# DeltaNet output norm and the second branch merge made one stage, in a one-core hybrid encoder kernel

## The reference, cut to what matters

```
o_b, s_gdn_new = gdn_recurrence(qb, kb, vb, beta, log_g, s_gdn)
o_b = rmsnorm(o_b, p['gdn_norm_w']) * jax.nn.silu(gb.reshape(B, T, GDN_HEADS, GDN_DV).astype(f32))
y_b = o_b.reshape(B, T, GDN_V).astype(h.dtype) @ p['w_br_b']
g_a, g_b, g_c = jnp.split(jax.nn.sigmoid(h @ p['w_gate'] + p['b_gate']), 3, axis=-1)
out = (g_a * y_a + g_b * y_b + g_c * y_c) @ p['w_out']
```

## Time and profile before

| | us |
|---|---|
| median of three runs | 2665.25 |
| lowest and highest run | 2663.41, 2666.01 |
| span of the profiled execution (its own time) | 2667.1 |
| TensorE busy | 2248.3 (84%) |
| VectorE busy | 758.6 (28%) |
| ScalarE busy | 417.9 (16%) |
| GpSimd busy | 188.9 (7%) |

### The profile page before, as it was taken

One profiled execution on the slowest core, in us unless ns is written; L12 is line 12 of the kernel. 1 busy time (PEld: TensorE's weight loads), 2 busy tenths in 40 slices (PEclk: granted clock), 3 DMA queues, 4 the chain that ended last, 5 costly groups with the idle time before them and its releaser, 6 DMA issues. The chain is left out here.

```text
span 2667.1 us, 27006 instructions
## 1 busy us (share of the span) xinstructions
PE 2248.3 (84%) x10591; PEld 1501.7 (56%) x10591; DVE 758.6 (28%) x1560; ACT 417.9 (16%) x929; POOL 188.9 (7%) x225
## 2 busy tenths in 40 slices
PE   4928698989999699799838999949969928999985
PEld 2215565755544466466417888836634417788772
DVE  1115265021020611023393444421113331111116
ACT  3001211110031400011222111140001101111112
POOL 0000000000000000000002211100000030000005
PEclk9968798579999899899968999969989969999997
DMA  6620212211200111111510000011141009999976
GB/s 223 224 40 2 35 34 14 1 48 40 58 0 0 29 29 40 20 32 40 9 1 16 9 9 1 1 36 36 35 162 56 32 13 354 350 351 353 348 259 215
DMA packets 227881, 237.03 MB, mean 89 GB/s; under 512 B 64976, under 2 KB 186160, under 8 KB 227776
## 3 DMA queue, kind: packets, MB, share of 16 engines
q1 hardware_dynamic: 218916, 206.32, 27.5%
q0 software_dynamic: 8880, 29.51, 3.0%
HBM read 207.87 MB, written 26.62 MB: 88 GB/s over the span
## 5 line engine op out<-in xcount | busy, mean ns | idle before, releaser
L2428 PEld LDWEIGHTS ex_ps<-ex_xt,ex_w_in 128*128 128x128 f32 x2048 | 236.0, 194 | 18.4 <-issue 14.8
L2428 PE MATMUL ex_ps<-ex_xt,ex_w_in 128*128 128x128 f32 x2048 | 236.3, 277 | 3.2 <-DMA ex_w_in<-in_w_exp_up 3.2
L1402 PE MATMUL cv_ps<-h,cv_w 128*128 128x364 f32 (+1 forms) x576 | 177.9, 472 | 17.1 <-DMA cv_w<-in_w_in 17.1
L1402 PEld LDWEIGHTS cv_ps<-h,cv_w 128*128 128x128 f32 x576 | 110.1, 192 | 83.9 <-DMA cv_w<-in_w_in 17.7
L2076 PE MATMUL pj_ps<-pj_w_out,mix 128*128 128x512 f32 (+1 forms) x288 | 127.0, 600 | 23.5 <-DMA pj_w_out<-in_w_out 23.5
L927 PE MATMUL b_gate_ps<-h,b_merge_w 128*128 128x364 f32 (+1 forms) x384 | 122.7, 473 | 7.1 <-DMA b_merge_w<-in_w_br_b 7.1
L927 PE MATMUL a_gate_ps<-h,a_merge_w 128*128 128x364 f32 (+1 forms) x384 | 122.9, 474 | 6.6 <-DMA a_merge_w<-in_w_br_a 6.6
L2439 PE MATMUL ex_ps<-ex_w_down,ex_hid 128*128 128x512 f32 x256 | 118.2, 605 | 8.1 <-DVE ex_hid L2514 5.9
L675 PE MATMUL s_ps<-h,s_w_gate 128*128 128x364 f32 (+1 forms) x384 | 117.3, 468 | 0.8 <-ACT s_before L726 0.8
L2076 PEld LDWEIGHTS pj_ps<-pj_w_out,mix 128*128 128x128 f32 (+1 forms) x288 | 53.2, 187 | 92.0 <-issue 67.9
L927 PEld LDWEIGHTS b_gate_ps<-h,b_merge_w 128*128 128x128 f32 x384 | 73.7, 192 | 51.8 <-DMA b_merge_w<-in_w_br_b 7.2
(11 more groups left out here) (442 smaller groups left out, 3095.1 us busy)
## 6 DMA issues: line engine op xcount, KB each, us to landing
ex_w_in<-in_w_exp_gate SPq DMA_DIRECT2D x32, 1024.0 KB, 8.3
ex_w_in<-in_w_exp_up SPq DMA_DIRECT2D x32, 1024.0 KB, 10.9
ex_w_down<-in_w_exp_down SPq DMA_DIRECT2D x32, 1024.0 KB, 9.9
ada_w<-in_w_ada SPq DMA_DIRECT2D x12, 2048.0 KB, 7.9
ys_dram<-ex_y SPq DMA_DIRECT2D x32, 512.0 KB, 10.0
cv_w<-in_w_in SPq DMA_DIRECT2D x12, 512.0 KB, 4.5
x_tiles<-in_x_prompt SPq DMA_DIRECT2D x1, 4096.0 KB, 15.5
s_w_gate<-in_w_gate SPq DMA_DIRECT2D x8, 512.0 KB, 3.9
```

What stands on the lines that cost most here:

```text
L1402: last = nc.tensor.matmul(ps[n][:, 0:width], w[:, j % 2, k], g.h[:, k, at:at + width], start=k == 0, stop=k == KD - 1)
L2428: last = nc.tensor.matmul(ps[2 + b][:, P * m:P * m + P], w_in[:, b, m // 2, k, P * (m % 2):P * (m % 2) + P], xt[:, b, k], start=m == 0 and ...
```

## The change

The two stages `stage_gdn_out` and `stage_merge` for branch B become one, `stage_gdn_merge`, with one barrier fewer. Its instructions are those of the two stages, with these differences. The 36 squares with their sums move into the core: ScalarE takes those of tile i-2 in tile i between the second decay exp and the power2 copies, and those of tiles 7 and 8 at its end. They write to `g.row_sel` and to the space of `g.gdn_ba`. The core's weight tile `w_gate` outlives it, and SP loads the first two column blocks of the merge's gate weights into it when gate jobs 27 and 36 are done. In the new stage ScalarE takes the root first and Silu after it. TensorE does the gate products of block 0, pieces 0 and 1, then the 9 transposes, then piece 2, then the branch products of block 0. Blocks 1 to 7 are written out without a loop, in the order of before. Gate and branch weights have buffers of their own; the gate weights of j are loaded after the gate products of j-2, branch weights after its branch products. The transposes use five PSUM banks, three of them those of the branch products.

```diff
         q_state = x[1]
         state = [sb(f"state{b}") for b in range(2)]
-        w_gate = sb("w_gate", [P, 2, KD, P])
+        w_gate = g.w_gate
+        square = g.row_sel[:, 0:P]
...
                 sp.dma_start(w_gate[:, c % 2], gate_view[:, :, P * c:P * c + P]).then_inc(S[f"gate_w{c % 2}"], 16)
+            merge_view = rows_view(d["w_gate"][0])[:, :, D:2 * D]
+            for j in range(2):
+                sp.wait_ge(S["gate_psum"], NT * (j + 3))
+                sp.dma_start(w_gate[:, j], merge_view[:, :, P * j:P * j + P]).then_inc(g.merge_loaded[j], 16)
...
+            def sum_squares(i):
+                n = P if i < NT - 1 else CHUNK
+                act.wait_ge(S["o_out"], i + 1)
+                for h in range(HEADS):
+                    q = HEADS * i + h
+                    if q:
+                        act.wait_ge(S["squared"], q)
+                    nc.scalar.activation(square[0:n], g.gdn_v[0:n, i, DV * h:DV * h + DV], ACT.Square,
+                                         accum_out=g.gdn_ssq[0:n, q:q + 1]).then_inc(S["squared"], 1)
+
             for i in range(NT):
...
                 nc.scalar.activation(decay[:], ps[2][:], ACT.Exp).then_inc(S["dec_exp"], 1)
+                if i >= 2:
+                    sum_squares(i - 2)
                 for r, (to, bank) in enumerate(((power2, 2), (power2_t, 3))):
...
+            sum_squares(NT - 2)
+            sum_squares(NT - 1)
...
+def stage_gdn_merge(nc, g, d):
...
+            def load_br(j):
+                sp.dma_start(w_br[:, j % 2], br_view[:, :, P * j:P * j + P]).then_inc(br_loaded[j % 2], 16)
+
+            sp.dma_start(bias[:], d["b_gate"][0].rearrange("(b k p) -> b p k", p=P, b=3)[1],
+                         allow_slow_non_contiguous=True).then_inc(bias_loaded, 16)
+            sp.dma_start(norm_col[:], d["gdn_norm_w"][0].rearrange("(p o) -> p o", o=1), allow_slow_non_contiguous=True).then_inc(loaded, 16)
+            load_br(0)
+            load_br(1)
+            for j in range(2, KD):
+                sp.wait_ge(gate_psum, 3 * (j - 1))
+                sp.dma_start(g.w_gate[:, j % 2], gate_view[:, :, D + P * j:D + P * j + P]).then_inc(g.merge_loaded[j % 2], 16)
+                sp.wait_ge(br_psum, 3 * (j - 1))
+                load_br(j)
+
+        @block.tensor
+        def _(pe):
+            def gates(j, n):
+                at, width = PIECES[n]
+                if n == 0:
+                    pe.wait_ge(g.merge_loaded[j % 2], 16 * (j // 2 + 1))
+                if j:
+                    pe.wait_ge(gate_done, 3 * (j - 1) + n + 1)
+                for k in range(KD):
+                    last = nc.tensor.matmul(gate_ps[n][:, 0:width], g.w_gate[:, j % 2, k], g.h[:, k, at:at + width],
+                                            start=k == 0, stop=k == KD - 1)
+                last.then_inc(gate_psum, 1)
+
...
+            def turn(i):
+                n = tokens(i)
+                pe.wait_ge(gated_o, i + 1)
+                if i >= 5:
+                    pe.wait_ge(branch_done, i - 4)
+                for h in range(HEADS):
+                    last = nc.tensor.transpose(turn_ps[i % 5][:, P * h:P * h + n], g.gdn_v[0:n, i, DV * h:DV * h + DV], g.ident[0:n, 0:n])
+                last.then_inc(turned, 1)
+
+            gates(0, 0)
+            gates(0, 1)
+            for i in range(NT):
+                turn(i)
+            gates(0, 2)
+            pe.wait_ge(branch_done, NT)
+            for n in range(3):
+                branch(0, n)
+            for j in range(1, KD):
+                for n in range(3):
+                    gates(j, n)
+                    branch(j, n)
+
+        @block.scalar
+        def _(act):
+            act.wait_ge(pads, 1)
+            nc.scalar.activation(std[:], g.gdn_ssq, ACT.Sqrt, scale=1.0 / DV, bias=g.eps[:]).then_inc(std_done, 1)
+            for i in range(NT):
+                nc.scalar.activation(swish[:, i], g.gate_rows(i), ACT.Silu).then_inc(swish_done, 1)
+
+            def sigmoid(j, n):
+                at, width = PIECES[n]
+                act.wait_ge(gate_psum, 3 * j + n + 1)
+                if j:
+                    act.wait_ge(gated, 3 * (j - 1) + n + 1)
+                nc.scalar.activation(gate[:, n, 0:width], gate_ps[n][:, 0:width], ACT.Sigmoid, bias=bias[:, j:j + 1]).then_inc(gate_done, 1)
+
+            act.wait_ge(loaded, 16)
+            for i in range(NT):
+                n = tokens(i)
+                act.wait_ge(turned, i + 1)
+                act.wait_ge(swish_done, NT)
+                nc.scalar.activation(g.branch[:, :, P * i:P * i + n], turn_ps[i % 5][:].rearrange("p (h t) -> p h t", h=HEADS)[:, :, 0:n],
+                                     ACT.Copy, scale=norm_col[:, 0:1]).then_inc(branch_done, 1)
+            act.wait_ge(bias_loaded, 16)
+            for j in range(KD):
+                for n in range(3):
+                    sigmoid(j, n)
+
...
+            g.gdn_ssq = g.gdn_ba[:].rearrange("p i c -> p (i c)")[:, 0:NT * HEADS]
             stage_gdn_in(nc, g, d, out)
+            g.w_gate = sb("gdn_w_gate", [P, 2, KD, P], inner)
+            g.merge_loaded = [inner.enter_context(nc.semaphore(f"merge_b_loaded{b}")) for b in range(2)]
             stage_gdn(nc, g, d, out)
-            stage_gdn_out(nc, g, d)
-        stage_merge(nc, g, d, "b", 1, False)
+            stage_gdn_merge(nc, g, d)
+
```

More of the change, by code:

```diff
@@ L1539, in stage_gdn @@
                  "p2_psum p2 p4_psum p4 x2_psum x2 x3_psum x3 p16_psum p16 x4_psum x4 p32_psum p32 x5_psum x5 p64_psum p64 x6_psum x6 "
-                 "gate_w0 gate_w1 gate_psum gate_out wk_psum wk u_psum qs_psum u_out ds_psum state o_psum qs_out o_out stored state_in").split()
+                 "gate_w0 gate_w1 gate_psum gate_out wk_psum wk u_psum qs_psum u_out ds_psum state o_psum qs_out o_out squared stored state_in").split()
         S = {n: sem(n) for n in names}
@@ L2658, in _, with sb, sem, tokens @@
             finish(NT - 1)
+def stage_gdn_merge(nc, g, d):
+    with ExitStack() as ctx:
+        def sb(name, shape):
+            return ctx.enter_context(nc.sbuf_tensor("gm_" + name, shape, F32))
+        def sem(name):
+            return ctx.enter_context(nc.semaphore("gm_" + name))
+        swish = sb("swish", [P, NT, BR])
+        std = sb("std", [P, NT * HEADS])
+        norm_col = sb("norm_col", [P, 1])
+        w_br = sb("w_br", [P, 2, KB, P])
+        bias = sb("bias", [P, KD])
+        gate = sb("gate", [P, 3, PW])
+        loaded, std_done, rstd_done, swish_done, gated_o, turned, branch_done, pads = (sem(n) for n in (
+            "loaded std_done rstd_done swish_done gated_o turned branch_done pads").split())
+        bias_loaded, gate_psum, br_psum, gate_done, gated, added = (sem(n) for n in (
+            "bias_loaded gate_psum br_psum gate_done gated added").split())
+        br_loaded = [sem(f"br_loaded{b}") for b in range(2)]
+        gate_ps = [ctx.enter_context(nc.psum_tensor(f"gm_gate_ps{b}", [P, 512], F32)) for b in range(3)]
+        br_ps = [ctx.enter_context(nc.psum_tensor(f"gm_br_ps{b}", [P, 512], F32)) for b in range(3)]
+        more_ps = [ctx.enter_context(nc.psum_tensor(f"gm_more_ps{b}", [P, 512], F32)) for b in range(2)]
+        turn_ps = more_ps + br_ps
+        block = ctx.enter_context(nc.Block())
+        gate_view = rows_view(d["w_gate"][0])
+        br_view = rows_view(d["w_br_b"][0])
+        def tokens(i):
+            return P if i < NT - 1 else DEC
+        @block.sync
+        def _(sp):
+            def load_br(j):
[22 more added lines that the diff above has]
+                last.then_inc(gate_psum, 1)
+            def branch(j, n):
+                at, width = PIECES[n]
+                if n == 0:
+                    pe.wait_ge(br_loaded[j % 2], 16 * (j // 2 + 1))
+                if j:
+                    pe.wait_ge(gated, 3 * (j - 1) + n + 1)
+                for k in range(KB):
+                    last = nc.tensor.matmul(br_ps[n][:, 0:width], w_br[:, j % 2, k], g.branch[:, k, at:at + width],
+                                            start=k == 0, stop=k == KB - 1)
+                last.then_inc(br_psum, 1)
+            def turn(i):
[25 more added lines that the diff above has]
+            def sigmoid(j, n):
+                at, width = PIECES[n]
+                act.wait_ge(gate_psum, 3 * j + n + 1)
+                if j:
+                    act.wait_ge(gated, 3 * (j - 1) + n + 1)
[11 more added lines that the diff above has]
+                    sigmoid(j, n)
+        @block.vector
+        def _(dve):
+            nc.vector.memset(g.gdn_ssq[DEC:P, HEADS * (NT - 1):], 1.0).then_inc(pads, 1)
+            dve.wait_ge(std_done, 1)
+            nc.vector.reciprocal(std[:], std[:]).then_inc(rstd_done, 1)
+            dve.wait_ge(rstd_done, 1)
+            for i in range(NT):
+                n = tokens(i)
+                dve.wait_ge(swish_done, i + 1)
+                for h in range(HEADS):
+                    o = g.gdn_v[0:n, i, DV * h:DV * h + DV]
```

(12 more changed lines are left out.)

## The result

The changed kernel took 2628.39 us (median of 4 runs, 2625.76 to 2629.65) against 2665.43 us of the kernel before on the same chip (4 runs): 37.0 us less, a ratio of 0.9861 (95% interval 0.9847 to 0.9875). 2630.0 was predicted.

A forecast was written before the change was run, and what follows sets the result against it. ScalarE, VectorE, DMA and TensorE work one after the other, so TensorE's standstill between core and column block 1 counts. Starting that block 35.3 us earlier gives 2665.25 - 35.3 = 2630.0 us; own range 2627 to 2633, wider range 2625.5 to 2638.

The forecast's parts named there:

- The mechanism: Between core's last matmul and merge's column block 1, TensorE's standing still is what counts; that block starts 35.3 us earlier.
- Part 1, the squares: In the core, ScalarE's idle 7.24 us a tile covers 1.73 of squares: cost 0; 15.58 us leave the serial path.
- Part 2, the barrier: Between core and new stage: barrier takes 0.4 us after ScalarE ends, so the stage starts at T = 1750.8.
- Part 3, the weights: Merge's first gate weights, loaded during the core, land before the state store; the 6.54 us DMA wait goes whole.
- Part 4, the stage: New stage on TensorE: gate pieces, transposes (4.0 us), branch products; column block 1 at T + 27.8, 1.76 for low clock.
- a clock below 1 beyond the first 4 us of the stage: Sign of being wrong: TensorE's clock in the new stage still below full speed after its first 4 us.
- Part 5: Merge's column blocks 1 to 7: taking the loop away gives 0, bounds 0 to 1.4 us.
- Changed tables: In the core, squares and exps need different function tables: 2.2 us lost, 7.7 without slack; chance 0.11.
- The squares on the core's path: In the core, ScalarE's delay by squares is passed on: up to 12.1 us, total 2642.0; chance 0.04.
- Late weights: In the new stage, TensorE still waits up to 6.5 us for gate weights, total 2636.5; chance 0.02.
- The clock that doesn't come back: In the merge, TensorE stays at 1.2 GHz; all instructions low would be 140 us slower, 2806; chance 0.02.
- TensorE starting warm: In the new stage, TensorE starts at full clock: 1.8 us more gained; counted inside the forecast's 0.80.

The follow-up runs named there:

- the squares alone: Kernel before with only the 36 squares taken inside the core, output norm and merge still two stages: 2652.56 us against 2666.78, one run each.
- two rounds of them: Changed kernel with the squares of tiles 0 to 6 taken twice over: 36.96 us between the outputs of two tiles, as before.
- the squares put back: Changed kernel with its squares back at the head of ScalarE's list in the new stage: 43.3 us from core's last matmul to column block 1.
- the run kept busy: Changed kernel with 12 unused products added behind TensorE's last work in the core: 2623.56 us against 2665.11 before, ratio 0.9847.
- the empty block: Changed kernel with a stage in which no engine does anything, and its barrier, behind the merged one: expert stage 389.5 us, against 388.0 changed.
- changed, again: Changed kernel, unaltered, profiled and timed a second time: 2626.79 us, ratio 0.9858 to the kernel before.
- weights late: Changed kernel with gate weights of column blocks 0 and 1 loaded in the new stage, not the core: 38.3 us from core's last matmul to block 1.

## Why the prediction was right, point by point

**The mechanism** held: what counts is TensorE's standing still. The gap shrank by 34.4 us where 35.3 was the sum. From the core's first product on, the two profiles differ by 36.7, close to the 37.0 of the medians: 34.4 are the gap and 1.8 the expert stage, 1.3 lie behind the experts (74.1 us before, 72.8 changed), and 0.1 and 0.6 are lost in the core and between column block 1 and the experts. So the measured time came within 1.6 us of the forecast by luck in part: the gap fell 0.9 short, and stages that had no term gave more than that.

**Part 1, the squares:** nothing in the core, as taken; the step is shown from both sides, by the squares alone (core 340.7) and by two rounds of them (36.96 a tile).

**Part 2, the barrier:** T was to be 2.95 us behind the last matmul and was 2.82. ScalarE was the last, as said, and the barrier took 0.27, where 0.4 was taken.

**Part 3, the weights:** the second load was issued at 1721.24, 9.7 us before the state's store, and TensorE's first matmul had no DMA in front of it.

**Part 4, the stage:** this is where the sum was 0.9 off, and the term is the clock. I took the 1.76 us of the first column block before; it was 12.59 - 9.80 = 2.8. The prediction had named a clock below 1 beyond the first 4 us of the stage as a sign of being wrong, and it came, at 5.5 us; the range let it run only from -1.8 to 0. The same event measured 1.7 in the kernel with the squares put back and 1.8 before, so one row was no bound; the run kept busy, which had it at 0, shows that the term is the clock's. The transposes took 3.98 (4.0 said), the third gate piece 4.94 (4.8 between the times given, 4.90 by its price), and the copies ended at 1766.7, 3.1 us before the branch products, where I had 1.9. The branch products took 7.32 (7.3).

**Part 5:** 0 for the loop taken away: 154.96 us for the seven blocks before and after.

**The range.** The bounds that the prediction lists add up to 2624.6 to 2632.3, not to 2627 to 2633: its lower end leaves out part of what it lists. The measured 2628.39 lies in both. And it took the 2667.1 us for the profiled execution's own time, 1.85 above the median; that is the span, and in the runs of before that have both, the time is 1.9 to 3.4 longer. The forecast is taken off the median and doesn't hang on it.

**The rivals.** Changed tables: not there, and when forced, free. The squares on the core's path: not with two rounds of them. Late weights: not there, and 6.6 us if they were. The clock that doesn't come back: it came back after 5.5 us. TensorE starting warm: no, but worth 2.4 us when forced.

**What the prediction had no term for** is the expert stage's 1.8 us and the 1.3 behind it. With the empty block 73.8 us lay behind the experts, 1.0 more than changed; but with the squares put back it was 74.0 without any empty block, so the cause of this part is open.

## What to carry to other kernels

Where a chain runs through engines in turn, sum up how long the engine that bounds the kernel stands still, and look for its own independent work to put in front of what it waits for: here squares moved into another engine's idle time, an early load and an order were worth 12, 7 and 7 us when each was taken away again, and the whole change 34. Here work added to ScalarE's list was free as long as it fitted the idle time behind it, which the trace shows, and for 1.0 us more. Compare two profiles by a distance inside them and not by their spans: the start and the end of this kernel scatter by more than several of the effects.

## What the runs showed that I had not expected

- The clock's fall and rise vary between places. It fell 0.3 us (empty block) to 1.6 us (changed, again) after the core's last matmul, and about 5 us after TensorE stopped when the squares were put back (1.00 until 1762, 0.84 for the 2 us after). It rose 3.0 us (squares put back) to 6.1 us (weights late) after the new stage's first matmul, and 5.5 in the changed kernel. The price of one cold start was 1.7 to 2.8 us.
- In the core a function table's load of 1.28 us ran ahead of the wait of the instruction that needs it; it cost nothing 6 times over.
- One block less in the program sped up an unchanged loop by 0.10 to 0.13 us a round.
